# First norm and attention projection of a hybrid encoder layer: one interleaved stage made two

## What is computed

```python
h = rms_norm(x, g_mix[l])              # y = x * rsqrt(mean(x*x) + eps), times gain
proj = h @ w_in[l]                     # columns: RWKV part, q (512), k (128), v (128)
q = rms_norm(q.reshape(B, T, ATTN_Q_HEADS, HEAD_DIM), q_gain)
k = rms_norm(k.reshape(B, T, ATTN_KV_HEADS, HEAD_DIM), k_gain)
...
bias = rel_bias[t5_bucket(rel)]        # rel = k_off - q_off, 128 x 384 for each of 8 heads
```

## Time and profile before

| | us |
|---|---|
| median of 3 runs | 3527.59 (3523.97 to 3529.44) |
| the profiled execution | 3525.42 |
| its span, first to last instruction | 3523.6 |
| PE busy in the span | 3072.8 (87%) |
| DVE busy | 1546.6 (44%) |
| ScalarE (ACT) busy | 1071.4 (30%) |
| POOL busy | 785.8 (22%) |

### The profile page before, as it was taken

One profiled execution on the slowest core, in us unless ns is written; L12 is line 12 of the kernel. 1 busy time (PEld: TensorE's weight loads), 2 busy tenths in 40 slices (PEclk: granted clock), 3 DMA queues, 4 the chain that ended last, 5 costly groups with the idle time before them and its releaser, 6 DMA issues. The chain is left out here.

```text
span 3523.6 us, 64121 instructions
## 1 busy us (share of the span) xinstructions
PE 3072.8 (87%) x26764; PEld 2465.0 (70%) x26764; DVE 1546.6 (44%) x1959; ACT 1071.4 (30%) x2041; POOL 785.8 (22%) x937
## 2 busy tenths in 40 slices
PE   5777998998472799999699779999999999799999
PEld 2545556886242789899466558888888888688887
DVE  2555552333355455453344374444444444333333
ACT  2333552111342344444324231111111111222222
POOL 2343551000235667663123150000000000000000
PEclk7888999999785999999899989999999999899999
DMA  4222112331346333321465231111111111522331
GB/s 109 90 87 64 37 37 50 73 74 48 122 180 225 100 108 108 108 79 40 153 198 181 90 122 39 52 50 52 48 48 48 48 48 42 225 89 56 95 96 36
DMA packets 214174, 313.19 MB, mean 89 GB/s; under 512 B 63257, under 2 KB 138393, under 8 KB 210874
## 3 DMA queue, kind: packets, MB, share of 16 engines
q1 hardware_dynamic: 212506, 308.74, 27.7%
q10 hardware_dynamic: 1440, 1.18, 0.1%
HBM read 208.16 MB, written 101.71 MB: 88 GB/s over the span
## 5 line engine op out<-in xcount | busy, mean ns | idle before, releaser
L91 PE MATMUL up_p<-h_hi,up_w_hi 128*128 128x512 f32 x1408 | 550.4, 391 | 40.5 <-DVE h_lo L1956 37.5
L92 PE MATMUL up_p<-h_lo,up_w_hi 128*128 128x512 f32 x1408 | 549.6, 390 | 0.0
L93 PE MATMUL up_p<-h_hi,up_w_lo 128*128 128x512 f32 x1408 | 549.3, 390 | 0.0
L91 PEld LDWEIGHTS up_p<-h_hi,up_w_hi 128*128 128x128 f32 x1408 | 265.2, 188 | 97.9 <-issue 42.9
L1908 ACT COPY up_raw<-up_p 128x512 f32<-128x512 f32 x176 | 103.2, 588 | 749.7 <-PE up_p L93 749.6
L93 PEld LDWEIGHTS up_p<-h_hi,up_w_lo 128*128 128x128 f32 x1408 | 265.4, 189 | 55.5
L92 PEld LDWEIGHTS up_p<-h_lo,up_w_hi 128*128 128x128 f32 x1408 | 265.6, 189 | 55.2
L91 PE MATMUL down_p<-down_act_hi,down_w_hi 128*128 128x512 f32 x704 | 275.0, 391 | 22.9 <-DVE down_act_lo L2113 22.9
L1966 DVE TENSOR_SCALAR up_con<-up_raw,vecs_sb 128x2048 f32<-128x2048 f32 x44 | 59.3, 1347 | 515.8 <-ACT up_raw L1908 515.8
L92 PE MATMUL down_p<-down_act_lo,down_w_hi 128*128 128x512 f32 x704 | 274.8, 390 | 0.0
L93 PE MATMUL down_p<-down_act_hi,down_w_lo 128*128 128x512 f32 x704 | 274.6, 390 | 0.0
(11 more groups left out here) (232 smaller groups left out, 6294.5 us busy)
## 6 DMA issues: line engine op xcount, KB each, us to landing
rec_inp<-gate_chunks SPq DMA_DIRECT2D x64, 512.0 KB, 3.5
up_w<-in_w_up SPq DMA_DIRECT2D x44, 512.0 KB, 4.0
act_out<-up_con SPq DMA_DIRECT2D x22, 1024.0 KB, 4.3
down_act<-act_out SPq DMA_DIRECT2D x88, 256.0 KB, 3.2
gate_chunks<-gates_out SPq DMA_DIRECT2D x4, 4096.0 KB, 11.8
first_w<-in_w_attn SPq DMA_DIRECT2D x24, 512.0 KB, 3.7
rkv_chunks<-rwkv_project_mix SPq DMA_DIRECT2D x12, 1024.0 KB, 6.4
down_w<-in_w_down SPq DMA_DIRECT2D x22, 512.0 KB, 13.3
```

The source lines that it names most:

```text
L91: pe.matmul(out, w_hi, x_hi, start=start, stop=False)
L92: pe.matmul(out, w_hi, x_lo, start=False, stop=False)
L93: return pe.matmul(out, w_lo, x_hi, start=False, stop=stop)
```

## The change

first_block is taken apart. start_block does the norm, writes h_hi and h_lo for all 2048 tokens, and makes and stores the bias rows. It is closed with end_phase. Then attn_project_block does the projection. In the first, x comes as one DMA of 2 MB a quarter from the second quarter on, into one of two buffers; ScalarE and DVE wait for a whole quarter; scaling by the root and the gain is one DVE instruction into a small buffer of two, from which ScalarE makes the high and DVE the low part; POOL has no work. In the second, the items go by tile and then by quarter, so each of the six weight tiles is loaded and split once, in eight pieces of 128x128 that follow the products of the previous tile's last quarter; DVE makes the low part. Queries are gathered as a whole tile of 2048 tokens and stored by one DMA of 1 MB a tile. The bias rows are stored behind the last load of x.

The diff, cut to its core (only added code; what goes is first_block as a whole):

```diff
+def norm_programs(K, S, x, loaded, gain, sq, inv, scaled, p_ss, hi, lo):
+    at = lambda t, k, n: t[:, k, n * NT:(n + 1) * NT]
+    def act_program(act):
+        def square(n, k):
+            g = n * KD + k
+            if k == 0:
+                loaded(act, n)
+            if g >= 2:
+                act.wait_ge(S["summed"], g - 1)
+            K.nc.scalar.activation(sq[:, g % 2], x(k, n), ACT.Square).then_inc(S["squared"], 1)
+        def root(n):
+            act.wait_ge(S["summed"], (n + 1) * KD)
...
+        for k in range(KD):
+            square(0, k)
+        root(0)
+        for n in range(TN):
+            for k in range(KD):
+                if n + 1 < TN and k < KD // 2:
+                    square(n + 1, 2 * k)
+                    square(n + 1, 2 * k + 1)
+                if n + 1 < TN and k == KD // 2:
+                    root(n + 1)
+                act.wait_ge(S["scaled"], n * KD + k + 1)
+                K.nc.scalar.copy(at(hi, k, n), scaled[:, k % 2]).then_inc(S["high"], 1)
...
+    def dve_program(dve):
+        def low(g):
+            k, n = g % KD, g // KD
+            dve.wait_ge(S["high"], g + 1)
+            K.nc.vector.tensor_tensor(at(lo, k, n), scaled[:, k % 2], at(hi, k, n).bitcast(F32),
+                                      ALU.subtract).then_inc(S["low"], 1)
+        for n in range(TN):
+            dve.wait_ge(S["rooted"], n + 1)
+            K.nc.vector.reciprocal(inv[:, n % 2], inv[:, n % 2]).then_inc(S["inverted"], 1)
...
+            for k in range(KD):
+                g = n * KD + k
+                if g >= 2:
+                    dve.wait_ge(S["low"], g - 1)
+                K.nc.vector.scalar_tensor_tensor(out=scaled[:, k % 2], in0=x(k, n), scalar=K.vec(gain, k),
+                                                 in1=inv[:, n % 2], op0=ALU.mult,
+                                                 op1=ALU.mult).then_inc(S["scaled"], 1)
+                if g >= 1:
+                    low(g - 1)
...
+def start_block(nc, K):
...
+        xt = sb("xt", [P, 2, KD, NT])
...
+        def loaded(eng, n):
+            if n == 0:
+                eng.wait_ge(S["const_in"], 32)
+            eng.wait_ge(S[f"x_in{n}"], 16 * KD if n == 0 else 16)
...
+                for n in range(1, TN):
+                    if n >= 2:
+                        sp.wait_ge(S["scaled"], (n - 1) * KD)
+                    sp.dma_start(xt[:, n % 2], K.d["xT"][:, :, n * NT:(n + 1) * NT]).then_inc(
+                        S[f"x_in{n}"], 16)
                 sp.wait_ge(S["bias_copied"], 1)
+                sp.dma_start(K.bias_rows, row[:, :].unsqueeze(1).to_broadcast([AH, P, 512])).then_inc(
                     S["bias_out"], 16)
+                sp.wait_ge(S["bias_out"], 16)
...
+def attn_project_block(nc, K):
...
+                def save(m):
+                    sp.wait_ge(S["normed"], (m + 1) * TN)
+                    sp.dma_start(K.q_dram[:, m], q[:, m % 2]).then_inc(S[f"q_saved{m % 2}"], 16)
+                for m in range(QK + 1):
+                    if m >= 1:
+                        sp.wait_ge(S["w_lo"], KD * m)
+                    sp.dma_start(w[:, :, :], K.d["w_attn"][m]).then_inc(S["w_in"], 16)
+                    if m >= 2:
+                        save(m - 2)
...
+                for m in range(QK + 1):
+                    for n in range(TN):
+                        g = m * TN + n
+                        if g >= 2:
+                            pe.wait_ge(S["copied"], g - 1)
+                            if g - 2 < VG:
+                                pe.wait_ge(S["squared"], g - 1)
+                        toks = slice(n * NT, (n + 1) * NT)
+                        for k in range(KD):
+                            if n == 0:
+                                pe.wait_ge(S["w_lo"], m * KD + k + 1)
+                            mm = product(pe, p_proj[:, g % 2], w_hi[:, k], w_lo[:, k], K.h_hi[:, k, toks],
+                                         K.h_lo[:, k, toks], k == 0, k == KD - 1)
+                            if n == TN - 1 or k == KD - 1:
+                                mm.then_inc(S["projected"], 1)
+                        if 1 <= g <= VG:
+                            sums(g - 1)
+                        elif g > VG:
+                            turn_v(g - 1 - VG)
...
+                def split(m):
+                    act.wait_ge(S["w_in"], 16 * m + 16)
+                    for k in range(KD):
+                        if m >= 1:
+                            act.wait_ge(S["projected"], (m - 1) * STEPS + TN - 1 + k + 1)
+                        nc.scalar.copy(w_hi[:, k], w[:, k]).then_inc(S["w_hi"], 1)
+                split(0)
+                for g in range(VG + TN):
+                    n = g % TN
+                    act.wait_ge(S["projected"], product_done(g))
+                    if g >= 2:
+                        if g - 2 < VG:
+                            act.wait_ge(S["normed"], g - 1)
+                            act.wait_ge(S["summed"], g - 1)
+                        else:
+                            act.wait_ge(S["turned"], g - 1 - VG)
                     nc.scalar.copy(raw[:, g % 2], p_proj[:, g % 2]).then_inc(S["copied"], 1)
+                    if g < VG:
+                        nc.scalar.activation(sq[:, g % 2], p_proj[:, g % 2], ACT.Square).then_inc(
                             S["squared"], 1)
+                        if n == TN - 2:
+                            split(g // TN + 1)
+                        act.wait_ge(S["summed"], g + 1)
+                        nc.scalar.activation(inv[:, g % 2], p_ss[:, g % 2], ACT.Sqrt, scale=1.0 / HD,
+                                             bias=K.vec("eps")).then_inc(S["rooted"], 1)
...
+                for g in range(VG):
+                    m, n = g // TN, g % TN
+                    if n == TN - 2:
+                        split(m + 1)
+                    dve.wait_ge(S["rooted"], g + 1)
+                    nc.vector.reciprocal(inv[:, g % 2], inv[:, g % 2]).then_inc(S["inverted"], 1)
...
+                    if n == 0 and 2 <= m < QK - 1:
+                        dve.wait_ge(S[f"q_saved{m % 2}"], 16 * (m // 2))
+                    nc.vector.scalar_tensor_tensor(
+                        out=to[:, n * NT:(n + 1) * NT], in0=raw[:, g % 2], scalar=gain,
+                        in1=inv[:, g % 2], op0=ALU.mult, op1=ALU.mult).then_inc(S["normed"], 1)
...
     with hold("h_hi", wide, F32R) as K.h_hi, hold("h_lo", wide, F32R) as K.h_lo:
+        start_block(nc, K)
         with hold("k_t", [P, T]) as K.k_t, hold("v_tok", [P, NB, P]) as K.v_tok:
-            first_block(nc, K)
+            attn_project_block(nc, K)
             attention_block(nc, K)
```

More of the change, by code:

```diff
@@ L88, in product @@
+NORM_SEMAPHORES = ["squared", "summed", "rooted", "inverted", "scaled", "high", "low"]
 def product(pe, out, w_hi, w_lo, x_hi, x_lo, start, stop):
@@ L93, in product @@
     return pe.matmul(out, w_lo, x_hi, start=False, stop=stop)
[L96 to L101, removed]
+def start_block(nc, K):
     with ExitStack() as ctx:
[L103 to L111, removed]
-        sq = sb("sq", [P, 2, NT])
[L113 to L142, removed]
@@ L166, in _ @@
                     S["bias_out"], 16)
[L168 to L177, removed]
@@ L178, in _ @@
-                slots(sp, body)
-                for b in range(2):
-                    sp.wait_ge(S[f"q_saved{b}"], 16 * TN * (QK - 1) // 2)
+                sp.wait_ge(S["bias_out"], 16)
+            @block.scalar
+            def _(act):
+                programs[0](act)
             @block.tensor
             def _(pe):
[L184 to L222, removed]
@@ L234, in _ @@
             @block.scalar
             def _(act):
[L236 to L246, removed]
@@ L248, in high @@
-                def high(n, ks):
-                    for k in ks:
-                        done(act, "scaled", n * KD + k + 1)
-                        nc.scalar.activation(K.h_hi[:, k, toks(n)], xt[:, k], ACT.Copy,
-                                             scale=K.vec("g_mix", k)).then_inc(S["high"], 1)
-                def split(g):
-                    done(act, f"w_in{g % 2}", 16 * (g // 2 + 1))
-                    done(act, "projected", g - 1)
-                    nc.scalar.copy(w_hi[:, g % 2], w[:, g % 2]).then_inc(S["w_hi"], 1)
@@ L272, in take, with copy_v @@
-                def take(g):
-                    done(act, "projected", g + 1)
-                    if g == 0:
-                        done(act, "bias_row", 1)
-                    if g == 0 or g == 1:
-                        done(act, "bias_out", 16)
-                    if is_qk(g - 2):
-                        if (g - 2) % MT < QK - 1:
-                            before = sum(1 for q in range(g - 1) if q % 2 == g % 2 and q % MT < QK - 1)
-                            done(act, f"q_saved{g % 2}", 16 * before)
-                        done(act, "normed", qk_count(g - 2) + 1)
-                    elif g >= 2:
```

(22 more changed lines are left out.)

191 lines of the change are left out of this document (101 added, 90 removed).

## The result

The changed kernel took **3489.73 us** (median of 5 runs, 3485.02 to 3502.46), the kernel before, timed beside it, 3527.59 (5 runs, 3522.34 to 3530.75). The ratio is 0.9898, 95% interval 0.9875 to 0.9921: about 1% faster, clear of noise, inside the forecast range and 3.6 us under the forecast. The profiled execution took 3489.73, its span is 3487.9 against 3523.6. The attention stage begins at 275.12 instead of 311.15, 36.0 us sooner; the spans differ by 35.7, so in this pair of executions all of the gain lies ahead of that mark.

The account below looks back on a forecast made before the run. The prediction took chains between engines to bound first_block. Attention starting at 276.8 instead of 311.15 gains 34.3 us: 3525.4 - 34.3 = 3491.1, on the median's footing 3493.3; own range 3484 to 3503, with rivals 3478 to 3511.

Parts of the forecast that it names:

- bias store: End of start_block: rows issued behind x3 at 63, moving 2.10 MB at 50 GB/s in 42 us, done at 115.7.
- stage 1: start_block (norm, split of h, bias row, no products): computation through at 102, the bias rows ending it near 116.
- stage 2: attn_project_block: dense products with items 6.34 us apart, 151.9 us in sum, PE ending at 273.4.
- First reciprocal: Start of start_block: waiting for all eight x0 loads shifts the reciprocal from 18.22 to 23.4.
- Two of the eight sums cold: Sums of squares in start_block: two of a quarter's eight run at the low clock, 1.70 us instead of 0.86.
- PE stays at the low clock: Rival for start_block: all sums at 1.70 us, 13.6 us a quarter instead of 8.6, giving 3503; chance 0.14.
- not the end: Rival: the bias transfer does not end start_block, which ends with computation at 102, giving 3479.6; chance 0.13.
- chain rival: Rival for attn_project_block: items wait on one another and last 11.5 us, 104 us more, giving 3597; chance 0.04.
- tail: End of attn_project_block: copy 0.6, transposes 0.8, copy_v 0.6, barrier 1.4, so attention starts at 276.8.
- Chains between engines bound the stage, not one engine: Claim on old first_block: quarters cost 68.5 us, items 11.53 us apart with next squares mixed in, 6.34 unhindered.
- 180 us: Old first_block: 311 us against 131.5 us of pure products; the rest is other work and waiting that reordering can win.
- rule weighed in the prediction: Trainium skill's DMA rule for the bias rows: some 2 us plus bytes at 436 GB/s, 6.8 us, ending start_block at 102.

Follow-up runs that it names:

- experiment 5: Changed kernel with x by slices and wide bias store, bias row's matmuls moved behind quarter 0's sums: 3470.0 us; with filler matmuls on PE too: 3476.24 us.
- experiment 4: Changed kernel with x loaded in 256 KB slices: 3487.06 us; both edits, with bias rows also stored from 128 partitions behind x1: 3473.49 us.
- experiment 3: Changed kernel, one execution each: narrow bias store ahead of x2, attention at 281.87; store from 128 partitions in the same place, attention at 272.92.
- Experiment 1: Kernel before, with only the bias rows laid on 128 partitions and stored from there: 3505.0 us, ratio 0.9922.

## Why the prediction was right

**The order of events was as written.** x0 as a whole delays the first squares, two waits for x, the bias store ends stage 1, no wait of PE in stage 2, items in an even rhythm, later stages unchanged. **The time was right partly because errors cancelled:**
- First reciprocal 23.4, measured 25.31. The step moved the old chain by the wait for x0 and left out that the change also moves the bias row's matmuls: in the kernel before they stood behind the first quarter's sums (at 17.22), now they stand ahead. The first square was there at 12.6, the first sum began at 14.63, 2.0 us later:
```profile
17.22 1.02 PE L228 MATMUL first_p_row<-first_raw,first_relb 32*8 32x512 f32 x2
```
```profile
11.12 1.87 PE L223 MATMUL start_p_row<-start_onehot,start_relb 32*8 32x512 f32 x2 [11.12 <-DMA start_relb<-in_rel_bias]
...
14.63 9.83 PE L129 MATMUL start_p_ss<-start_sq,consts_sb 128*128 128x512 f32 x16
```
  With x by slices, where the squares are there sooner, the same place cost 5.0 us at the mark (experiment 5).
- Quarter 0 scaled at 40, measured 40.5: the late start was won back, since none of the sums of quarter 1 were cold (granted clock 1.00 in 28 to 36), where two were forecast. x2 landed at 51.46 instead of 49.8. The 2 MB loads x2 and x3 took 10.9 and 11.4 us from issue to landing, not the 9.8 and 9.6 that were taken from the earlier trace rows; together this is 2.9 us.
- Quarter 1 ends at 66.2 instead of 63, computation at 108.6 instead of 102. Of these 6.6 us, 0.5 come from quarter 0 and 2.9 from the loads; the other 3.2 lie in the work behind them. "Two of the eight sums cold" was close behind x2 and too few behind x3, where three squares in a row stand 1.7 us apart (80.38, 82.08, 83.79). How much of the 3.2 us this is, the runs don't separate. The squares behind x2:
```profile
54.25 0.63 ACT L100 ACTIVATE start_sq<-start_xt 128x512 f32<-128x512 f32 x1 [1.14 <-PE start_p_ss L129]
55.96 0.63 ACT L100 ACTIVATE start_sq<-start_xt 128x512 f32<-128x512 f32 x1 [1.08 <-PE start_p_ss L129]
```
PE had stood idle for 15.7 us; its sums come 1.70 us apart first, and the granted clock of 51 to 63 is 0.75. The rival "PE stays at the low clock" was true only for the first sums behind x0, x2 and x3.
- **The bias store** was put behind x3: 9.4 + 42.3 + 1 = 52.7 us from the issue of x3. Both were issued within 0.8 us of each other, and it took 112.35 - 66.78 = 45.6. The two ran beside each other: 66 to 78 shows 150 to 275 GB/s, more than the rows' 51. With only the last slices of x3 ahead of it the same store took 42.8 (experiment 4, 62.77 to 105.5), so the whole of x3 ahead added some 3 us and not 9.4. This overlap is the step that the forecast had wrong by most. So the stage ended at 112.35, not 115.7, and the store was 3.7 us behind the computation, not 14. The rival "not the end" missed by that much; experiment 3 made it true.
- **Stage 2**, first product to the end of the last: 272.4 - 118.0 = 154.4 against 151.9. Items start 6.45 us apart (ScalarE's roots at 138.60 and 145.05), not 6.34: the matmuls stand 0.233 us apart instead of 0.228, 24 x 24 x 0.005 = 2.9 us. Why is open. The head sum is 6.45 - 24 x 0.233 = 0.85, as taken (0.86). The chain rival fell: an item never came near 8.0.
- The tail took 2.7 us instead of 3.4. In sum, measured less forecast: -3.4 for stage 1, +2.5 for stage 2, -0.7 for the tail are, rounded, the 1.7 us between 276.8 and 275.12. Inside stage 1 the luck is larger: the computation freed the bias store 3.8 us late (66.78 for 63), and the store was 7.1 us shorter than forecast. The last 2 us of the 3.6 are how medians stand to single executions.

**What the argument had wrong is the reason, not the time.** "Chains between engines bound the stage, not one engine" put the gain down to the taking apart. Experiment 1 got 27.5 of the 36.0 us with the old chains in place. The 30.9 us wait stood in the earlier trace rows and was read as one wait among several; but it was a single wait of ScalarE, whose program feeds all other engines, and its removal came through almost whole (27.5 of 30.9). The taking apart gives the remaining 8.5, net of what new stage 1 pays: 21 us of waits for x, the row ahead of the sums, and the store. (With the wide store in both kernels it gives 283.69 - 272.92 = 10.8.) With these costs taken out (experiments 4 and 5) it gives 283.69 - 249.55 = 34 us over the old stage without its stall. How this splits between POOL's part, the weight split and the order of the norm, no run shows. So the 180 us that the prediction found over the pure products were partly reachable by order, 61.6 us of them at the mark.

On the rule weighed in the prediction: the rows took 45.6 us from issue to landing, and showed 51 GB/s in the stretch from 78 to 105. The Trainium skill, "DMA: Bandwidth & Descriptors", section "Anatomy of one DMA", would give 6.8; it has this fit for DMAs that GpSimd issues, and these are issued by SyncE. The trace disagrees with it for a source of eight partitions, and the measurement decides. From 128 partitions the same bytes took 8.2 us (experiment 1) and 7.3 (experiment 4, both edits), not far from it. The number of busy engines explains a factor of about two: the share went from 0.46 to about 1, the time to less than a fifth. Why the narrow store moves so little on each engine that it keeps busy, the runs don't show.

## What to carry to other kernels

Look at the DMA share and the rate of a broadcast store. The one here, from eight partitions, kept the share at 0.46 and moved 51 GB/s, and a load behind it in its queue came late as well: moving it moved the stall, spreading its source over 128 partitions removed it. Before a stage is rebuilt, take away its longest single wait alone and see what is left, since a long wait of the engine that feeds all others hides how well the chains would run. When a stage is written anew, check what stands ahead of the main chain in each engine's program: the row of a small table there cost 5.0 us in experiment 5, and the description of the change does not name that move. A load that waits for a whole buffer can be cut into slices that go as their places come free; here that took the computation's end from 108.6 to 94.6.

## What the runs showed of the hardware that was not expected

- 2.10 MB from eight partitions: share 0.46, 51 GB/s, 42.8 us from issue to landing with little ahead; from 128 partitions: share 1.00 to 1.03, 296 to 385 GB/s with the next loads included, 7.3 to 8.2 us. With x3 beside them, 15.9 us at up to 402 GB/s.
- A 2 MB load issued in the middle of the narrow store in the same queue landed after 23.0 us (ScalarE waited 22.4 us), one issued just ahead of it after 11.4, while the store took only some 3 us longer for it.
- The same fp32r matmul, 128x512, ran 0.233 us after the one before in the items of the new stage 2, at a clock of 1.00, and 0.228 in the later RWKV projection. Double-buffered weights did not change it (median duration 396 ns, against 389 in the earlier trace rows). The cause is open.
- PE's first sums stood 1.7 us apart behind x0, x2 and x3, after PE had idled 11 to 16 us (behind x0 with the row's two matmuls in between), and not after the 1.4 and 2.9 us of idling at quarter 1's sums. Five filler matmuls, 3.4 us in all, did not hold the clock through the sums behind them (0.79 in 42 to 50).
